# Tokens on partitions and 512-column moving weights in the feed-forwards of a two-model stack

## Chip, cores and metric

The kernel runs on one core of a Trainium2 chip. The time is device microseconds for one launch; three runs gave 2978.11 to 2979.29 us, median 2978.93. All names and lines below are those of the kernel before.

## What is computed

Two layers of one transformer-like block, then its final norm, then two layers of a second block, on 256 tokens of width 1024, all in float32.

```python
def rms_norm(x, g):
    xf = x.astype(jnp.float32)
    y = xf * lax.rsqrt(jnp.mean(xf * xf, axis=-1, keepdims=True) + EPS)
    return (y * g.astype(jnp.float32)).astype(x.dtype)
def swiglu(h, w_gu, w_down):
    gate, up = jnp.split(h @ w_gu, 2, axis=-1)
    return (jax.nn.silu(gate) * up) @ w_down
# first block, per layer (D_FF = 2816)
x = x + 0.5 * swiglu(rms_norm(x, ffn1_norm[l]), ffn1_w_gu[l], ffn1_w_down[l])
z = rms_norm(x, mix_norm[l]) @ w_in[l]   # dilated attention, HGRN2 recurrence, two gates
x = x + merged @ w_mix_out[l]
x = x + cross_attention(rms_norm(x, xattn_norm[l]), rms_norm(mem, mem_norm[l]), ...)
x = x + 0.5 * swiglu(rms_norm(x, ffn2_norm[l]), ...)
# second block, per layer: mod = silu(c) @ w_ada + b_ada gives nine rows of shift, scale, gate
x = x + 0.5 * g1 * swiglu_2(modulate(rmsnorm(x, norm_g[0]), sh1, sc1), ...)
x = x + g2 * (o @ w_out)                 # o: three attentions on a second projection
x = x + 0.5 * g3 * swiglu_2(modulate(rmsnorm(x, norm_g[2]), sh3, sc3), ...)
```

## The kernel before

Everything is transposed: the residual `x` is held as features on the 128 partitions, 8 blocks `k` of 128 features by 256 tokens. All weights come as one stream of 438 tiles of 128 x 2048 floats (1 MB). The queue SP loads tile `p` into a ring of four when tile `p-4` is done. `high` (L278, ACT) rounds it to `w_hi` (three buffers, so it waits until tile `p-3` is done), `low` (L287, DVE) writes the remainder over the ring. `triple` (L295, PE) makes each product from three fp32r matmuls (high x high, high x low, low x high). A tile is 48 matmuls: `project` (L310) has the weights as the stationary 128 x 128 operand and 256 tokens as the moving one; `project_tok` (L321) the reverse, with 256 weight columns moving. Each ends with a count on `tile_done`, which frees the ring.

A norm: `square` on ACT, `norm_pe` (ones-matmul over the 8 blocks, L366), Ln and Exp on ACT, a correction step `refine` on DVE over all 256 tokens, then scaled, high and low parts in quarters (`norm_dve` L393, `split_act` L354). PE waits for the first quarter of the next `h_hi`, `h_lo`.

A feed-forward (`ffn_pe` L425) has 11 chunks of 256 inner columns, 33 tiles: gate and up of chunk `i`, then down of chunk `i-1`. The inner product `g_f`, `g_hi`, `g_lo` is made by DVE (`gated` L541) in the transposed layout that down wants. The four output banks are cleared by zero matmuls and added to for the whole feed-forward. In seven of the eight DVE also does the modulation product (`ada_product` L487) with tiles that POOL loads. There are eight feed-forwards (FFN_A, FFN_B in each layer of the first block, FFN_C, FFN_D of the second). In FFN_B of both layers the rstd is applied late, to gate and up.

After FFN_A comes the mix. Its tiles are M_F (forget, 4), M_Q (4), M_I (value, 4), M_QK and so on. The evacuation of the fourth M_F tile starts a list on DVE (L1221 to L1264: reciprocal, scale, scan, arguments of the decay), with `low` calls written in between by hand; the order of every queue is written out in the code. After FFN_C comes Z_QI, ahead of each FFN_D the out projection Z_O, and the cross attention has M_OUT ahead and X_O behind.

## Time and profile before

| | |
|---|---|
| median of three runs | 2978.93 us |
| profiled execution | 2977.7 us, its span 2975.7 us |
| mean granted clock of PE | 0.985 of full speed |
| PE busy | 2874.4 us, 97% |
| DVE busy | 2036.3 us, 68% |
| ACT busy | 1315.9 us, 44% |
| DMA | 551 MB, mean 185 GB/s |

PE is TensorE, PEld its weight load, DVE VectorE, ACT ScalarE, POOL GpSimd, SP the queue that loads the stream. A busy PE is not PE at its peak, since matmul records overlap: the start-to-start distance tells the rate.

### The profile page before, as it was taken

What the parts mean: (1) busy time and instruction counts of PE and PEld (TensorE: products, weight loads), DVE (VectorE), ACT (ScalarE), POOL (GpSimd) and SP (SyncE); (2) the same over time, 40 slices, a digit from 0 to 9 for tenths busy, and PEclk for the clock granted to TensorE, in tenths of its full rate; (3) what the DMA queues carried; (4) which work ended last, traced back from release to release, by engine and by line L of the source; (5) the groups of instructions that cost most, each with busy time, mean ns of one, the idle gap of its engine ahead of it and who ended that gap; (6) DMA issues with size and microseconds to landing.
All of it is one profiled execution on the core that took longest, in us unless ns stands there. A gap on an engine that the chain in (4) does not pass through costs nothing.

```text
span 2975.7 us, 51299 instructions
## 1 busy us (share of the span) xinstructions
PE 2874.4 (97%) x22844; PEld 2806.2 (94%) x22844; DVE 2036.3 (68%) x2287; ACT 1315.9 (44%) x1303; POOL 206.6 (7%) x166
## 2 busy tenths in 40 slices
PE   7999999999999999999999998998999999999999
PEld 7999999999999999999999998997889999987999
DVE  6677876556677677876656776667866676778644
ACT  5334545444334344545444334335643343446432
POOL 0000420000000000420000000003000000030000
PEclk9999999999999999999999999999999999999999
DMA  7664433445665754433445665663246656542454
GB/s 274 240 227 156 155 125 133 154 148 202 241 241 212 250 204 170 142 134 123 163 148 214 243 238 184 241 227 128 86 178 246 236 215 253 184 141 72 156 183 143
DMA packets 79035, 551.09 MB, mean 185 GB/s; under 512 B 8544, under 2 KB 12000, under 8 KB 12896
## 3 DMA queue, kind: packets, MB, share of 16 engines
q1 hardware_dynamic: 67152, 464.98, 43.6%
q0 software_dynamic: 11664, 82.84, 7.3%
q8 instruction: 180, 2.95, 0.4%
q14 instruction: 39, 0.32, 0.0%
HBM read 546.74 MB, written 1.05 MB: 184 GB/s over the span
## 4 chain that ended last, share of the span: by engine, by line
PE 80%; DVE 13%; ACT 3%; issue 2%; POOL 2%; DMA 0%; DVEq 0%; POOLq 0%; SPq 0%; ACTq 0%
PE ps L298 73%; DVE ring_lo L292 3%; ACT w_hi L285 2%; PE ps L370 1%; PE ps L770 1%; POOL qk L1520 1%; DVE hk L1223 1%; POOL rope_a L1516 1%; DVE e L375 0%; PE ps L900 0%; PE ps L1610 0%; DVE e L1281 0%; DVE e L1280 0%; DVE e L397 0%; DVE a_hg L1301 0%
## 5 line engine op out<-in xcount | busy, mean ns | idle before, releaser
L292 DVE TENSOR_TENSOR ring_lo<-ring,w_hi 128x2048 fp32r<-128x2048 f32 x438 | 1009.5, 2307 | 649.2 <-ACT w_hi L285 645.6
L298 PE MATMUL ps<-h_hi,w_hi 128*128 128x256 f32 x4560 | 1312.5, 288 | 52.0 <-DVE h_lo L407 27.5
L298 PE MATMUL ps<-h_lo,w_hi 128*128 128x256 f32 x4560 | 1298.7, 285 | 0.0
L298 PE MATMUL ps<-h_hi,ring_lo 128*128 128x256 f32 x4560 | 1298.1, 285 | 0.0
L285 ACT ACTIVATE w_hi<-ring 128x2048 fp32r<-128x2048 f32 x438 | 836.7, 1910 | 807.5 <-PE ps L298 631.3
L298 PEld LDWEIGHTS ps<-h_hi,w_hi 128*128 128x128 f32 x4560 | 883.8, 194 | 63.7 <-issue 55.6
L298 PEld LDWEIGHTS ps<-h_lo,w_hi 128*128 128x128 f32 x4560 | 884.6, 194 | 2.9 <-issue 2.4
L298 PEld LDWEIGHTS ps<-h_hi,ring_lo 128*128 128x128 f32 x4560 | 883.8, 194 | 0.0
L298 PE MATMUL ps<-g_hi,w_hi 128*128 128x256 f32 x1408 | 398.5, 283 | 0.0
L298 PE MATMUL ps<-g_lo,w_hi 128*128 128x256 f32 x1408 | 398.5, 283 | 0.0
L298 PE MATMUL ps<-g_hi,ring_lo 128*128 128x256 f32 x1408 | 398.5, 283 | 0.0
L298 PEld LDWEIGHTS ps<-g_hi,w_hi 128*128 128x128 f32 x1408 | 270.3, 192 | 0.0
L298 PEld LDWEIGHTS ps<-g_lo,w_hi 128*128 128x128 f32 x1408 | 270.3, 192 | 0.0
L298 PEld LDWEIGHTS ps<-g_hi,ring_lo 128*128 128x128 f32 x1408 | 270.3, 192 | 0.0
L496 DVE CUSTOM_DVE_ANT_0 e<-e,val 128x1024 f32<-128x1024 f32 x154 | 181.9, 1218 | 0.0
L523 ACT ACTIVATE g_f<-ps 128x512 f32<-128x512 f32 x66 | 39.5, 598 | 209.5 <-PE ps L298 209.5
L298 PE MATMUL ps<-w_hi,h_hi 128*128 128x256 f32 x448 | 130.7, 292 | 0.0
L298 PE MATMUL ps<-ring_lo,h_hi 128*128 128x256 f32 x448 | 128.2, 286 | 0.0
L298 PE MATMUL ps<-w_hi,h_lo 128*128 128x256 f32 x448 | 128.1, 286 | 0.0
L484 POOL DMA_DIRECT2D e<-ada x77 | 40.6, 528 | 1205.8 <-DVE mod_sum L496 1049.4
L550 DVE TENSOR_TENSOR g_f<-g_f,ps 128x512 f32<-128x512 f32 x88 | 60.5, 687 | 69.6 <-PE ps L298 68.9
L298 PEld LDWEIGHTS ps<-w_hi,h_hi 128*128 128x128 f32 x448 | 87.6, 196 | 1.6 <-issue 1.6
(316 smaller groups left out, 3164.7 us busy)
## 6 DMA issues: line engine op xcount, KB each, us to landing
ring<-stream SPq DMA_DIRECT2D x438, 1024.0 KB, 4.8
...
```

The lines of the kernel that those rows point to most:

```text
L285: nc.scalar.activation(w_hi[:, p % HIGHS, :], ring[:, p % RING, :], ACT.Copy).then_inc(S.w_hi_ready, 1)
L292: nc.vector.tensor_tensor(ring_lo[:, p % RING, :], ring[:, p % RING, :], w_hi[:, p % HIGHS, :].bitcast(F32), ALU.subtract).then_inc(S.w_lo ...
L298: mm = nc.tensor.matmul(out, a, b, start=start and n == 0, stop=stop and n == 2, skip_group_check=group)
L370: mm = nc.tensor.matmul(ps[:, bank, 0:T], ones, sq[:, k, :], start=(k == 0), stop=(k == KD - 1))
L484: pool.dma_start(e_buf[(i + 1) % 2][:].rearrange("p k t -> p (k t)"), ada[l * 2 * PER_FFN + first + i]).then_inc(ada_loaded[(i + done) % 2 ...
L496: ins = nc.vector.tensor_tensor_reduce(part, part, silu_c, 1.0, 0.0, ALU.mult, ALU.add, mod_sum[:, at + n:at + n + 1])
L523: nc.scalar.activation(g_f[:, i % 2, :], ps[:, i % 2, :], ACT.Silu).then_inc(S.silu_done, 1)
L550: nc.vector.tensor_tensor(g_f[:, b, :], g_f[:, b, :], ps[:, 2 + b, :], ALU.mult).then_inc(S.hidden_step, 1)
L770: mm = nc.tensor.matmul(ps[:, 4 + 2 * g + j // 2, at:at + n], sta[:, hd, t * P:(t + 1) * P], right, start=True, stop=True)
L1223: ins = nc.vector.reciprocal(hk[:, hd, :], hk[:, hd, :])
L1516: nc.gpsimd.tensor_tensor(rope_a[:], part, cos1[:].unsqueeze(1).broadcast_to([P, 2, T]), ALU.mult).then_inc(S.pool_chain, 1)
L1520: nc.gpsimd.tensor_tensor(part, rope_a[:], turned[n % 2][:], ALU.add).then_inc(S.rope_done, 1)
```

## The change

`x` is held as two blocks of 128 tokens on partitions, 1024 features each, and so is the output. A norm sums squares within a partition (`accum_out`), rstd is one column per block, and gains, shifts and gates are rows broadcast to all partitions by POOL's DMAs (from memory; the modulation vector is written there first by `send_mods`). The scaled block is transposed by PE (`flip_x`, four 128 x 128 per half-row), copied to `h_hi` by ACT (`h_high`) and `h_lo` by DVE (`h_low`). All 256 tokens are no longer treated at once: block 0 runs ahead of block 1 (`cross_act`, `cross_dve`, `first_pair`, and `after` in `ffn_pe`).

In feed-forwards, the value projection and the out projections the activations are stationary and 512 weight columns move; a tile now holds 4 of 8 `k` blocks for 512 columns (`by_halves`), and two tiles make a projection. Gate and up of a chunk share a bank. The inner product comes out with tokens on partitions and is transposed by PE (`flip`), then split. The zero matmuls go. `out_pairs` does an out projection so: both blocks for the first 512 columns, then block 0, then block 1 for the rest. In the mix two value tiles go ahead of M_F, two stay behind M_Q.

The core of the diff, with eight columns of indentation taken off:

```diff
+def cross_act(act, n, base, p, late, ready=None):
+    def sq(q):
+        square(act, n, q, ready and ready[q])
+    sq(0)
+    sq(1)
+    if late:
+        h_high(act, n, 0, base)
+        h_high(act, n, 1, base)
+        nc.scalar.preload_act_table_set("natural_log_exp_and_others")
+        rstd_act(act, n, 0)
+    else:
+        rstd_act(act, n, 0)
+        h_high(act, n, 0, base)
+        h_high(act, n, 1, base)
+    if p >= 0:
+        act.wait_ge(S.tile_done, p + 1)
+    high(act, p + HIGHS)
+    sq(2)
+    sq(3)
+    if not late:
+        rstd_act(act, n, 1)
+    h_high(act, n, 2, base)
+    h_high(act, n, 3, base)
+    if late:
+        rstd_act(act, n, 1)
+    if p >= 0:
+        act.wait_ge(S.tile_done, p + 2)
+    high(act, p + 1 + HIGHS)
+def flip_x(pe, n, b, base):
+    for q in (2 * b, 2 * b + 1):
+        pe.wait_ge(S.h_scaled, nth(S.h_scaled, 4 * n + q + 1))
+        for j in range(4):
+            at = (4 * (q % 2) + j) * P
+            mm = nc.tensor.transpose(ps[:, base + q, j * P:(j + 1) * P], xs[:, b, at:at + P], ident)
+        mm.then_inc(S.xt_done, 1)
...
+def residual(dve, chain, q, bank, scale):
+    part = part_of(x, q)
+    if isinstance(scale, float):
+        nc.vector.scalar_tensor_tensor(out=part, in0=ps[:, bank, :], scalar=scale, in1=part,
+                                       op0=ALU.mult, op1=ALU.add).then_inc(S.x_ready, 1)
+    else:
+        chain(nc.vector.tensor_tensor(part_of(xs, q), ps[:, bank, :], row_of(ROW_GATE, q), ALU.mult))
+        nc.vector.tensor_tensor(part, part, part_of(xs, q), ALU.add).then_inc(S.x_ready, 1)
...
+def cross_dve(dve, chain, n, base, p, late, shift, row_count, into=None):
     def scaled(q):
+        if late:
+            ins = nc.vector.tensor_tensor(part_of(xs, q), part_of(x, q), row_of(ROW_GAIN, q), ALU.mult)
         else:
+            ins = nc.vector.scalar_tensor_tensor(out=part_of(xs, q), in0=part_of(x, q),
+                                                 scalar=rs[:, q // 2:q // 2 + 1], in1=row_of(ROW_GAIN, q),
+                                                 op0=ALU.mult, op1=ALU.mult)
+        if shift:
+            chain(ins)
+            ins = nc.vector.tensor_tensor(part_of(xs, q), part_of(xs, q), row_of(ROW_SHIFT, q), ALU.add)
+        ins.then_inc(S.h_scaled, 1)
+    def add(q):
+        if into:
+            into(q)
+            dve.wait_ge(S.x_ready, nth(S.x_ready, 4 * n + q - 3))
+    def tile_low(i):
+        low(dve, p + i + HIGHS)
+    if row_count == 0:
+        dve.wait_ge(S.first_row, 16)
+    else:
+        dve.wait_ge(S.row_loaded, 16 * row_count)
+    if late:
+        for q in range(2):
+            add(q)
+            scaled(q)
+        h_low(dve, n, 0, base)
+        h_low(dve, n, 1, base)
+        variance(dve, n, 0)
+        rstd_dve(dve, chain, n, 0, True)
+        tile_low(0)
+        for q in range(2, 4):
+            add(q)
+            scaled(q)
+        h_low(dve, n, 2, base)
+        h_low(dve, n, 3, base)
+        variance(dve, n, 1)
+        rstd_dve(dve, chain, n, 1, True)
+    else:
+        for b in range(2):
+            add(2 * b)
+            add(2 * b + 1)
+            if b == 1:
+                tile_low(0)
+            variance(dve, n, b)
+            rstd_dve(dve, chain, n, b)
+            scaled(2 * b)
+            scaled(2 * b + 1)
+            h_low(dve, n, 2 * b, base)
+            h_low(dve, n, 2 * b + 1, base)
+    tile_low(1)
+def first_pair(pe, p, n, base, banks, done=None):
+    pe.wait_ge(S.w_lo_ready, p + 1)
+    for b in range(2):
+        for k in range(KD):
+            if k % 4 == 0:
+                pe.wait_ge(S.h_ready, nth(S.h_ready, 4 * n + 2 * b + k // 4 + 1))
+            if b == 0 and k == 4:
+                pe.wait_ge(S.w_lo_ready, p + 2)
+            if b == 0 and k == 6:
+                flip_x(pe, n, 1, base)
+            mm = triple(ps[:, banks[b], :], both(h2, k, b * P, (b + 1) * P),
+                        weights(p + k // 4, (k % 4) * 512, (k % 4 + 1) * 512), k == 0, k == KD - 1)
+            if b == 1 and k % 4 == 3:
+                mm.then_inc(S.tile_done, 1)
+        if b == 0 and done is not None:
+            mm.then_inc(done, 1)
...
+def ffn_pe(pe, p0, f, n, base, between=None, after=None):
+    def gate_up(i, half, p, b):
+        for k in range(4):
+            mm = triple(ps[:, 2 * (i % 2) + b, :], both(h2, 4 * half + k, b * P, (b + 1) * P),
+                        weights(p, k * 512, (k + 1) * 512), half == 0 and k == 0, half == 1 and k == 3)
+        return mm
+    def flip(i, blocks):
+        for b in blocks:
+            pe.wait_ge(S.prod_done, nth(S.prod_done, 2 * (CHUNKS * f + i) + b + 1))
             for a in range(2):
+                mm = nc.tensor.transpose(ps[:, 2 * (i % 2), a * T + b * P:a * T + (b + 1) * P],
+                                         g_f[:, i % 2, b, a * P:(a + 1) * P], ident)
+        mm.then_inc(S.t_done, 1)
+    def down(i, b, p):
+        for h in range(2):
+            for a in range(2):
+                c = a * T + b * P
+                mm = triple(ps[:, 4 + 2 * b + h, :], both((g_hi, g_lo), i % 2, c, c + P),
+                            weights(p, a * D + h * 512, a * D + (h + 1) * 512), i == 0 and a == 0,
+                            i == CHUNKS - 1 and a == 1)
+            if i == CHUNKS - 1 and 2 * b + h < 3:
+                mm.then_inc(S.down_done, 1)
+        return mm
+    first_pair(pe, p0, n, base, (0, 1), S.gu_done)
+    if between:
+        between()
+    for i in range(1, CHUNKS):
+        p = p0 + 3 * i - 1
+        pe.wait_ge(S.w_lo_ready, p + 1)
+        for b in range(2):
+            mm = gate_up(i, 0, p, b)
+        mm.then_inc(S.tile_done, 1)
+        flip(i - 1, (0, 1))
+        pe.wait_ge(S.w_lo_ready, p + 2)
+        gate_up(i, 1, p + 1, 0).then_inc(S.gu_done, 1)
+        gate_up(i, 1, p + 1, 1).then_inc(S.tile_done, 1)
+        if i < CHUNKS - 1:
+            pe.wait_ge(S.g_ready, nth(S.g_ready, (CHUNKS + 1) * f + i))
+            pe.wait_ge(S.w_lo_ready, p + 3)
+            if i == 1 and f == 0 and between:
+                pe.wait_ge(S.mem_var, 1)
+            for b in range(2):
+                mm = down(i - 1, b, p + 2)
             mm.then_inc(S.tile_done, 1)
+    last, p = CHUNKS - 1, p0 + FFN_TILES - 2
+    flip(last, (0,))
+    pe.wait_ge(S.g_ready, nth(S.g_ready, (CHUNKS + 1) * f + last))
+    pe.wait_ge(S.w_lo_ready, p + 1)
+    down(last - 1, 0, p)
+    pe.wait_ge(S.g_ready, nth(S.g_ready, (CHUNKS + 1) * f + last + 1))
+    pe.wait_ge(S.w_lo_ready, p + 2)
+    down(last, 0, p + 1)
+    flip(last, (1,))
+    down(last - 1, 1, p).then_inc(S.tile_done, 1)
+    if after:
+        after()
+    pe.wait_ge(S.g_ready, nth(S.g_ready, (CHUNKS + 1) * f + last + 2))
+    down(last, 1, p + 1).then_inc(S.tile_done, 1)
...
+    silu(0, 0)
+    tile_high(0)
+    silu(0, 1)
+    tile_high(1)
+    if between:
+        between()
+    if row:
+        silu_row(act, row)
+    for i in range(1, CHUNKS):
+        if i >= 2:
+            tile_high(3 * i - 2)
+        act.wait_ge(S.t_done, nth(S.t_done, (CHUNKS + 1) * f + i))
+        nc.scalar.activation(g_hi[:, (i - 1) % 2, :], ps[:, 2 * ((i - 1) % 2), :],
+                             ACT.Copy).then_inc(S.ghi_ready, 1)
+        tile_high(3 * i - 1)
+        silu(i, 0)
+        silu(i, 1)
+        if i < CHUNKS - 1:
+            tile_high(3 * i)
+    last = CHUNKS - 1
+    for b in range(2):
+        act.wait_ge(S.t_done, nth(S.t_done, (CHUNKS + 1) * f + last + 1 + b))
+        nc.scalar.activation(halves_of(g_hi[:, last % 2, :])[:, :, b * P:(b + 1) * P],
+                             halves_of(ps[:, 2 * (last % 2), :])[:, :, b * P:(b + 1) * P],
+                             ACT.Copy).then_inc(S.ghi_ready, 1)
+        if b == 0:
+            tile_high(3 * last)
+def ffn_dve(dve, l, layers, p0, f, late, products=True, between=None):
+    def gated(i, b):
+        dve.wait_ge(S.silu_done, nth(S.silu_done, 2 * (CHUNKS * f + i) + b + 1))
+        up = ps[:, 2 * (i % 2) + b, T:2 * T]
+        g = g_f[:, i % 2, b, :]
+        if late:
+            ins = nc.vector.scalar_tensor_tensor(out=g, in0=up, scalar=rs[:, b:b + 1], in1=g,
+                                                 op0=ALU.mult, op1=ALU.mult)
+        else:
+            ins = nc.vector.tensor_tensor(g, g, up, ALU.mult)
+        ins.then_inc(S.prod_done, 1)
+    gated(0, 0)
     low(dve, p0 + HIGHS)
+    gated(0, 1)
+    low(dve, p0 + 1 + HIGHS)
     if between:
         between(0)
     if products:
         ada_product(dve, l, layers, PER_FFN * f, 0)
     for i in range(1, CHUNKS):
+        if i >= 2:
+            low(dve, p0 + 3 * i - 2 + HIGHS)
+        dve.wait_ge(S.ghi_ready, nth(S.ghi_ready, (CHUNKS + 1) * f + i))
+        nc.vector.tensor_tensor(g_lo[:, (i - 1) % 2, :], ps[:, 2 * ((i - 1) % 2), :],
+                                g_hi[:, (i - 1) % 2, :].bitcast(F32), ALU.subtract).then_inc(S.g_ready, 1)
+        low(dve, p0 + 3 * i - 1 + HIGHS)
+        gated(i, 0)
+        gated(i, 1)
         if i < CHUNKS - 1:
+            low(dve, p0 + 3 * i + HIGHS)
         if products:
             ada_product(dve, l, layers, PER_FFN * f, i)
         if between:
             between(i)
+    last = CHUNKS - 1
+    for b in range(2):
+        dve.wait_ge(S.ghi_ready, nth(S.ghi_ready, (CHUNKS + 1) * f + last + 1 + b))
+        at = (slice(None), slice(None), slice(b * P, (b + 1) * P))
+        nc.vector.tensor_tensor(halves_of(g_lo[:, last % 2, :])[at], halves_of(ps[:, 2 * (last % 2), :])[at],
+                                halves_of(g_hi[:, last % 2, :])[at].bitcast(F32),
+                                ALU.subtract).then_inc(S.g_ready, 1)
+        if b == 0:
+            low(dve, p0 + 3 * last + HIGHS)
...
+    first_pair(pe, MIX, 1, 4, (0, 1))
+    for n in range(2, 10):
         if n >= 3:
             pe.wait_ge(S.evac_done, nth(S.evac_done, n - 2))
-        (project_tok if n >= 8 else project)(pe, MIX + n, n % 3, h2)
+        project(pe, MIX + n, n % 3, h2)
+    for half in range(2):
+        project_half(pe, M_I1 + half, half, (10 % 3, 11 % 3), h2, 8)
...
-    ffn_dve(dve, l, 0, FFN_A, 0, between=once if l == 0 else None)
-    residual(dve, ffn_banks(dve, FFN_A, 0), 4, 0.5,
-             lambda b: gains(dve, 4, v_now[:, V1_MIX:V1_MIX + KD], b))
-    low(dve, MIX - 2 + HIGHS)
-    norm_dve(dve, chain, 1)
-    low(dve, MIX - 1 + HIGHS)
+    ffn_dve(dve, l, 0, FFN_A, 0, True, between=once if l == 0 else None)
+    cross_dve(dve, chain, 1, 4, FFN_A + FFN_TILES - 2, False, False, 4 * l + 1,
+              with_ready(dve, chain, ffn_ready(dve, FFN_A, 0), 4, 0.5))
     chain(nc.vector.tensor_copy(lb_now[:, 1, :], lb[:, l, :]))
     chain(nc.vector.tensor_scalar(lb_now[:, 0, :], lb_now[:, 1, :], -1.0, 1.0, ALU.mult, ALU.add))
     for n in range(4):
-        low(dve, M_F + n + HIGHS)
-    dve.wait_ge(S.evac_done, nth(S.evac_done, 4))
+        low(dve, MIX + n + HIGHS)
+    dve.wait_ge(S.evac_done, nth(S.evac_done, 6))
     chain(nc.vector.tensor_scalar(hk[:], hk[:], 1.0, None, ALU.add))
...
-    norm_pe(pe, 0, e_buf[0])
-    ffn_pe(pe, FFN_C, 0, 0)
-    norm_pe(pe, 1, e_buf[0])
+    if l == 0:
+        flip_x(pe, 0, 0, 4)
+    ffn_pe(pe, FFN_C, 0, 0, 4, after=lambda: flip_x(pe, 1, 0, 4))
+    flip_x(pe, 1, 1, 4)
```

## Rows read from the trace of the kernel before

**Rows 1.** The page: busy time of each engine.

```profile
PE 2874.4 (97%) x22844; PEld 2806.2 (94%) x22844; DVE 2036.3 (68%) x2287; ACT 1315.9 (44%) x1303; POOL 206.6 (7%) x166
```

**Rows 2.** The page: GB/s in 40 slices; engines' shares of the last chain.

```profile
GB/s 274 240 227 156 155 125 133 154 148 202 241 241 212 250 204 170 142 134 123 163 148 214 243 238 184 241 227 128 86 178 246 236 215 253 184 141 72 156 183 143
...
PE 80%; DVE 13%; ACT 3%; issue 2%; POOL 2%; DMA 0%; DVEq 0%; POOLq 0%; SPq 0%; ACTq 0%
```

**Rows 3.** Chain of waits, whole span: start us, length us, what, instructions.

```profile
21.10 7.86 PE ps L298 x48
...
216.91 3.47 PE ps L370 x16
...
225.03 25.53 PE ps L298 x192
...
720.88 184.31 PE ps L298 x1536
...
1792.79 3.47 PE ps L370 x16
...
1810.89 191.93 PE ps L298 x1584
...
2002.82 3.47 PE ps L370 x16
...
2011.42 13.58 PE ps L298 x96
...
2771.74 3.47 PE ps L370 x16
...
2780.34 191.94 PE ps L298 x1584
```

**Rows 4.** Groups by shape: count | busy us, mean ns | idle before.

```profile
L298 PE MATMUL ps<-h_hi,w_hi 128*128 128x256 f32 x4560 | 1312.5, 288 | 52.0 <-DVE h_lo L407 27.5 <-DVE h_lo L403 20.0 <-DVE ring_lo L292 2.6
...
L292 DVE TENSOR_TENSOR ring_lo<-ring,w_hi 128x2048 fp32r<-128x2048 f32 x438 | 1009.5, 2307 | 649.2 <-ACT w_hi L285 645.6
...
L285 ACT ACTIVATE w_hi<-ring 128x2048 fp32r<-128x2048 f32 x438 | 836.7, 1910 | 807.5 <-PE ps L298 631.3 <-DMA ring<-stream 176.0
...
L370 PE MATMUL ps<-e,con_sb 128*128 128x256 f32 x240 | 57.9, 396 | 12.9 <-ACT e L343 12.9
...
L343 ACT ACTIVATE e<-x 128x512 f32<-128x512 f32 x60 | 36.6, 625 | 34.0 <-DVE x L600 17.2 <-DVE x L604 14.0 <-DVE x L1536 2.8
...
L600 DVE SCALAR_TENSOR_TENSOR x<-ps,x 128x512 f32<-128x512 f32 x32 | 22.1, 692 | 28.4 <-PE ps L298 27.5
...
L348 ACT ACT_TABLE_LOAD x15 | 19.2, 1283 | 0.3
```

**Rows 5.** Timeline, PE, behind a gap: start us, length us, instruction.

```profile
2194.86 0.41 PE L298 MATMUL ps<-h_lo,w_hi 128*128 128x256 f32 x1
2195.07 0.41 PE L298 MATMUL ps<-h_hi,ring_lo 128*128 128x256 f32 x1
```

**Rows 6.** Timeline, a norm's matmuls ahead of the second block's layer 1.

```profile
2387.01 3.62 PE L370 MATMUL ps<-e,con_sb 128*128 128x256 f32 x16
```

**Rows 7.** Chain of waits, the list of DVE in the mix.

```profile
256.48 4.98 DVE hk L1223 x3
...
295.50 2.21 DVE ring_lo L292
...
297.85 11.76 PE ps L298 x96
```

**Rows 8.** Chain of waits, 440 to 700 us: four transposes.

```profile
645.20 0.44 PE ps L911 x4
```

**Rows 9.** The ring's DMAs: landing times.

```profile
DMA to landing us min/median/max: 4.6/4.8/13.0
```

**Rows 10.** Instructions on the tile prob: reading the accumulator.

```profile
L1129 ACT ACTIVATION_READ_ACCUMULATOR prob<-prob,small x16: 186/187/188, 639.7 to 1551.2; 128x1 f32 x16
```

More of the change, by code:

```diff
@@ L94, in tiles_1 @@
     at = l * TILES_1
-    return [at + t for t in (FFN_A, MIX, M_F, M_Q, M_I, M_QK, M_OG, M_YB, M_YA, M_KV0, M_OUT, M_KV1, X_Q, X_V, X_O,
+    return [at + t for t in (FFN_A, MIX, M_F, M_Q, M_I1, M_QK, M_OG, M_YB, M_YA, M_KV0, M_OUT, M_KV1, X_Q, X_V, X_O,
                              FFN_B)]
@@ L134 @@
 VEC_LB = VEC_2 + DEPTH * V2_W
[L135 to L136 removed]
+VEC_INV = VEC_LB + DEPTH * KD
 VEC_W = VEC_INV + 1
@@ L477, in ada_pool @@
+        def ada_pool(pool, l, first, done, free, row=False, then=None):
             for i in range(PER_FFN):
@@ L503, in silu_row, with ffn_act, silu, tile_high @@
             nc.scalar.activation(silu_c, silu_c, ACT.Silu).then_inc(S.silu_row, 1)
-        def ffn_late_act(act, p0, f, n, row):
-            for t in range(FFN_TILES - 1):
+        def ffn_act(act, p0, f, late, between=None, row=None):
+            def silu(i, b):
+                if late is not None and i == 0:
+                    act.wait_ge(S.rs_ready, 2 * late + b + 1)
+                if b == 0:
+                    act.wait_ge(S.gu_done, nth(S.gu_done, CHUNKS * f + i + 1))
+                else:
+                    act.wait_ge(S.tile_done, p0 + (2 if i == 0 else 3 * i + 1))
+                nc.scalar.activation(g_f[:, i % 2, b, :], ps[:, 2 * (i % 2) + b, 0:T], ACT.Silu,
+                                     scale=1.0 if late is None else rs[:, b:b + 1]).then_inc(S.silu_done, 1)
+            def tile_high(t):
@@ L1314, in one_dve @@
             args(0)
-            for n in range(1, 4):
-                low(dve, M_I + n + HIGHS)
+            for n in range(9, 12):
+                low(dve, MIX + n + HIGHS)
             for i in range(LEVELS + 1):
@@ new lines, in final_act @@
+        def final_act(act):
+            nc.scalar.preload_act_table_set("natural_log_exp_and_others")
+            for b in range(2):
+                square(act, 0, 2 * b)
+                square(act, 0, 2 * b + 1)
+                rstd_act(act, 0, b)
+        def final_dve(dve, chain):
+            dve.wait_ge(S.row_loaded, 16 * (4 * DEPTH + 2))
+            for b in range(2):
+                variance(dve, 0, b)
+                rstd_dve(dve, chain, 0, b)
+                for q in (2 * b, 2 * b + 1):
+                    nc.vector.scalar_tensor_tensor(out=part_of(x, q), in0=part_of(x, q), scalar=rs[:, b:b + 1],
+                                                   in1=row_of(ROW_GATE, q), op0=ALU.mult,
+                                                   op1=ALU.mult).then_inc(S.x_ready, 1)
@@ L2120, in ahead @@
                     vectors_two(chain, l + 1)
-            def first_gains(b):
-                if l < DEPTH - 1:
-                    gains(dve, 12, parts[1], b)
-            ffn_dve(dve, l, DEPTH, FFN_D, 1, products=l < DEPTH - 1, between=ahead)
-            residual(dve, ffn_banks(dve, FFN_D, 1), 4, parts[8], first_gains)
+            low(dve, Z_O + HIGHS)
+            low(dve, Z_O + 1 + HIGHS)
+            cross_dve(dve, chain, 2, 0, Z_O + 2, False, True, row_count + 6,
+                      with_ready(dve, chain, z_ready, 0, None))
@@ L2129, in two_pool @@
+            ffn_dve(dve, l, DEPTH, FFN_D, 1, False, products=l < DEPTH - 1, between=ahead)
+            into = with_ready(dve, chain, ffn_ready(dve, FFN_D, 1), 4, None)
+            if l < DEPTH - 1:
+                cross_dve(dve, chain, 3, 4, FFN_D + FFN_TILES - 2, False, True, row_count + 9, into)
+            else:
+                dve.wait_ge(S.row_loaded, 16 * (row_count + 7))
+                for q in range(4):
+                    into(q)
         def two_pool(pool, l):
+            sent = 1 + 3 * l
```

775 lines of the change are left out of this document (346 added, 429 removed).

## Prediction

> **What bounds the kernel now.** I read the totals first: PE is busy for 2874 of 2975.7 us, DVE for 2036, ACT for 1316 [rows 1]; the chain that ended last gives PE 80% and DVE 13% [rows 2]. So PE's rate and PE's gaps are what a change can win. Three things are to be seen.
>
> The rate: in a feed-forward 1536 matmuls of 256 columns take 184.31 us, 0.1200 us each, no gap between them [rows 3]. A tile of 1 MB is 48 of them, 5.76 us. Each has its own weight load beside it, and a record lasts 288 ns, so they overlap [rows 4]. Is 0.120 the stream of 256 columns, or the load of the 128 x 128 operand? Two rows say the load. At the low clock (1.2 GHz) the same matmuls start 0.21 us apart [rows 5], which is 256 columns at one a cycle with nothing added. And where a record streams twice as long, the sixteen of L370, the last starts about 3.62 - 0.40 = 3.22 us after the first [rows 4, 6]: 0.215 us each, 0.213 of it columns.
>
> The gaps: between streams PE stands about 5 us and spends 3.5 on the ones-matmul of the norm. Norm to stream takes 216.91 to 225.03 (8.1 us), 2002.82 to 2011.42 (8.6), 2771.74 to 2780.34 (8.6), and 18.1 where the final norm lies between two blocks (1792.79 to 1810.89); the streams behind them are 1.9 to 2.5 us longer than their count at 0.120, in part at the low clock [rows 3, 5]. Five more gaps repeat these patterns.
>
> The projections after the first feed-forward of each layer: PE is hardly idle, but DVE's list (reciprocals L1223, scan, weight remainders) runs from the end of the four forget tiles, 225.03 + 25.53 = 250.6, to the remainder for tile MIX+12, which ends at 297.7, and PE starts that tile at 297.85 [rows 7]. That wait ends last there.
>
> **The change, part by part.** The sum is made against the profiled execution, 2977.7 us.
>
> 1. *512 columns.* 296 of the 438 tiles (8 x 33 of the feed-forwards; 8 value tiles; 24 of the out projections) go from 48 x 0.120 to 24 matmuls. Bounds for one: 0.215 [rows 6] and 0.240, twice the 256-column pace [rows 3]. I take 0.216, near the lower end, as its row has the same stream length beside a load. 7104 x 0.024 = -170.5 us. Fixed cost of 0.0133 per matmul instead would make it 0.227 (+76 us on my sum).
> The Trainium skill, "TensorE: Matmul & The Clock Gate", section "Back-to-back issue gap", gives N/2.4 + 2.5 ns for one matmul behind another: 215.7 ns at 512, which the trace's 0.215 fits, but 109 ns at 256, where the trace has 120. Its section on LDWEIGHTS puts a load at P/1.2, 107 ns, which would not hold a 256-column stream back; by that rule the extra 11 ns would be a cost per matmul and the gain would be the smaller one (about 2965 us).
>
> 2. *Transposes of the inner part.* 4 per chunk, 44 per feed-forward, 352 in all. Four take 0.44 us between matmuls of other kinds [rows 8]: 352 x 0.109 = +38.3 us, all on PE, nothing hides them. Bounds 0.107 and 0.13 a piece: 37.7 to 46.
> The wait on them is covered in the steady part: flip(i-1) wants a product finished 10 us before, and its copy (0.6) and remainder (0.7) lie under the second half of gate-up, 5.2 us. Per chunk (15.98 us) DVE has three remainders 6.9, two products 0.9, one g_lo 0.7, the modulation product 2.6 = 11.1, ACT 7.1. Weight tiles: load to landing 4.8, at most 13.0 [rows 9], high 1.91, low 2.3 [rows 4], in 3 x 5.18 = 15.6 us. Covered, except at the longest landings.
>
> The stream's rate rises from 4 MB in 17.28 us (243 GB/s) to 4 MB in 15.98 (262 GB/s); a slice with more, 274, stands in the page [rows 2]. New on POOL's queue are the rows for gain, shift and gate (0.5 MB each, one to three ahead of a crossing, in the block's second half behind a write of the modulation vector to memory), issued a feed-forward chunk or a dozen microseconds before DVE waits for them; a 1 MB load lands in 4.8, so I take nothing. If that cover is gone, a crossing waits up to one landing, 13 us [rows 9]. SP's queue keeps its order apart from the start, where weight tile 0 now goes ahead of half of x.
>
> 3. *End of a feed-forward.* DVE does gated(10,1), the modulation product (2.6) and only then g_lo of block 0, which down(10,0) waits for: DVE is free 3.7 us after gate-up ends, g_lo at 4.2, PE arrives at 2.9. Stall 1.3, in 7 of 8.
>
> 4. *Crossings.* The norm matmuls and the 5 us waits go; 16 transposes (1.75 us) come, and block 1 must be waited for in the middle of first_pair. I follow each queue in its order, prices from [rows 4]: residual 0.69, square 0.63 + accumulator 0.19 [rows 10], single-column steps 0.1 to 0.3 each, 1.3 together, scale 0.69. With t=0 at the end of down(10,0), feed-forward to mix:
> DVE must first do g_lo of block 1, which needs flip(10,1): 1.25. Residuals 2.65, square 3.5, rstd 4.8, scaled 5.45 and 6.15. PE has finished down(9,1) at 2.85 and waits 2.6; transposes; down(10,1) ends at 9.25, not 5.4. Block 1: residuals to 10.15, the weight remainder low(MIX+1), which the code puts ahead of the variance, to 12.45, rstd 13.6, scaled 14.3 and 15.0. PE does k 0-3 by 11.85, waits for that remainder, k 4-5 to 13.8, waits, transposes, and ends the pair at 22.0, against 5.4 + 10.4 bare. Overhead 6.2 + 1.3 = 7.5; before 8.1 + 2.5 = 10.6.
> The same bookkeeping, with these differences: *late* form (layer 0's last feed-forward to layer 1's first) scales at once but has table load 1.28 and high(tile 1) in front of k=4: 6.8 against 9.6, -2.8. *Gate and shift rows* (second block) double the residual and the scaling: 12.7 against 11.2 into FFN_C of layer 1; Z_O to FFN_D 13.0 against 10.5, twice. *FFN_C to Z_QI* has no first_pair to lie under: PE is through down(10,1) at 12.2 and block 1 is transposed only at 20.7; start 21.0, then 2.3 at the low clock: 19.2 against 10.7, +8.5, twice. *Final norm*: 18.2 against 20.0, -1.8. The crossings of M_OUT and X_O lie partly under other projections before and after; I take their sum as unchanged, +-3 each. *Start*: the tables' chain of DVE (7 us) moves from ahead of the first matmul to behind the first pair; first matmul about 16.5 instead of 21.1 [rows 3], but down(0) then waits for g_lo: +3. *End*: the last residual has two ops: +0.6.
> Sum without the mix: -2.8 +1.5 +5 +17 -1.8 +3 +0.6 = +22.5.
>
> 5. *Order of the mix.* Two value tiles are now ahead of the forget tiles, and DVE's list starts at the sixth evacuation. The list keeps its length: about 47.9 us from the last forget tile to low(MIX+12), Ln now behind tile MIX+10. From the bare end of the feed-forward: 1.3 + 3.85 + first pair 12.75 + four tiles 23.0 + 47.9 + two tiles 11.5 = 100.3 to the first level; before 216.91 to 309.6 = 92.7 [rows 3, 7]. +7.7 per layer, though four tiles there got shorter (4 x 0.576, which item 1 has credited already): +20 for both. PE's stalls appear at MIX+7 (3.2), MIX+8 (1.3), MIX+12 (9).
>
> Sum: 2977.7 - 170.5 + 38.3 + 22.5 + 20 = 2888. The runs' median is 1.2 above the profiled execution: **2889**. So the tiles give and about half of it is handed back.
>
> **Rivals.**
> A. *The block order pays in full*: each crossing costs its transposes and 2 us, no more. The nine gaps cost 104 us before, with the lengthened streams behind them; they would cost 9 x 3.75 = 34, a gain of 70 where my sum has a loss of 13 (-6.2 for the two ahead of the mix is inside its +20): 2889 - 83 = 2806. For it: the diff lets block 0's chain run under 5 us of matmuls. Against it: the chain I add up is longer than the cover, and part of it sits behind low() and g_lo on DVE. With only part of it, 2835.
> B. *A per-matmul cost*, 0.227: 2965. For it, the 13 ns at 256; against, the row of L370 [rows 6].
> C. *Crossings worse*: longer waits drop PE to the low clock more often (a first tile there takes 2.1 to 2.5 more [rows 3]); eight more of them and 1 to 2 us each: 2910 to 2935.
> D. *Slower than before*: the 512-column stream keeps the 256-column rate, 0.240 each. Then item 1 is nothing, and transposes and crossings remain: 2978 + 38 + 42 = 3059. It decides from 0.2286 us per matmul upwards (80.8/7104 = 0.0114 below 0.240). Against it: 0.21 at the low clock shows one column a cycle.
>
> **How the numbers follow.** Forecast 2889, its own range 2865 to 2915: 0.55. A (whole or part) 0.19, C 0.13, B 0.07, D 0.05, no change 0.01. The range 2835 to 2935 leaves out the lower half of A, B and D, about 0.2 together. Under 0.2% (6 us) no measurement here tells from no change; faster is the forecast, A, C and nearly all of B: 0.93; within 0.2% 0.02; slower D, 0.05.
>
> **What would show it.** Feed-forward matmuls 0.216 apart and 33 tiles plus transposes in about 176 us; PE's first tile of the mix ahead of a DVE list that ends where PE waits at MIX+7 and MIX+12; PE idle near 8 us ahead of Z_QI, with the low clock behind it; residual of block 0 on DVE behind g_lo. Wrong would be: starts 0.227 or more apart, or crossings in which PE waits less than 2 us.

## The result, and the profile after

The changed kernel takes 2990.1 us against 2978.2 us of the kernel before, five runs each: a ratio of 1.0043, 95% interval 1.0028 to 1.0058. It is slower, by more than the 0.2% that can be told from no change, where 2889 was forecast. The profiled execution spans 2987.7 us.

From the page: busy time of each engine, and the engines' shares of the chain that ended last.

```profile
PE 2817.1 (94%) x16040; PEld 2449.9 (82%) x16040; DVE 1976.3 (66%) x2205; ACT 1374.4 (46%) x1550; POOL 224.4 (8%) x197
...
PE 75%; DVE 15%; ACT 5%; issue 2%; DMA 2%; POOL 2%; SPq 0%; DVEq 0%; ACTq 0%; POOLq 0%
```

Beside [rows 1, 2]: PE does 57 us less with 6804 fewer records, and the span is 12 us longer, so PE stands about 70 us more. ACT, DMA and DVE have a larger share of the chain. A triple of matmuls is now L304, high L291, low L298, a transpose of the inner product (`flip`) L593, one of the scaled block ahead of a projection (`flip_x`) L406.

The rate, from the chain of waits (start us, length us, what, instructions), and the group of 512-column matmuls (count | busy us, mean ns of one):

```profile
777.05 16.38 PE ps L304 x72
793.86 16.36 PE ps L304 x72
```

```profile
L304 PE MATMUL ps<-w_hi,h_hi 128*128 128x512 f32 x1600 | 638.7, 399 | 11.9 <-DVE ring_lo L298 10.8 <-DVE h_lo L456 0.7
```

A chunk of a feed-forward is three tiles, 72 matmuls, and four transposes: 793.86 - 777.05 = 16.81 us, 16.36 / 72 = **0.2272 us** a matmul and 0.44 for the four. [Rows 3] had 17.28 for the same work; 15.98 was forecast. No gap lies inside these streams.

The waits of PE (released by: total us, times, longest):

```profile
PE ps L406 <- DVE e L470: 49.8, 22, 8.7
PE ps L304 <- DVE ring_lo L298: 36.2, 13, 9.2
PE ps L406 <- DVE e L463: 17.6, 5, 15.7
PE ps L304 <- DVE g_lo L750: 14.4, 5, 5.1
PE ps L406 <- DVE e L465: 8.4, 6, 2.5
PE ps L304 <- DVE g_lo L765: 4.6, 7, 0.7
```

L406 waits are the crossings (the stretch from one projection's last product through the residual and norm to the next one's first), 15.7 of them the start. The ring_lo waits are mostly the mix (3.4 and 9.3 in each layer). L765 is the end of a feed-forward. L750 is the first down product of a feed-forward (5.1, 2.1, 1.1, 2.9 and 3.2, in five of the eight), and the forecast had no such wait apart from the start. The chain through one of them, layer 0's second feed-forward:

```profile
732.47 8.83 DMA ring<-stream
...
741.41 1.92 ACT w_hi L291
...
743.36 0.97 DVE ring_lo L298
...
745.57 1.22 DVE e L667
...
747.94 0.61 DVE g_lo L750
...
748.60 11.22 PE ps L304 x48
```

Block order keeps weight tile p0 of the first pair in use until block 1 has passed through it (732.45). Only then is tile p0+4 asked for, and the first down product wants it 14 us later, at 746.5 (the pair's last twelve matmuls 2.7, gate-up 10.9, four transposes 0.4). It lands in 8.8, its high takes 1.9 and its remainder 2.3, and DVE does the modulation product (2.4) ahead of g_lo (0.6): 16 us, and PE starts at 748.6.

A crossing in which DVE sets the pace, FFN_C to Z_QI, on the same chain (1994 to 2030 us):

```profile
2006.15 1.11 PE ps L406 x4
2007.26 4.13 PE ps L304 x12
...
2012.93 2.29 DVE ring_lo L298
...
2019.36 1.11 PE ps L406 x4
...
2020.59 9.51 PE ps L304 x66
```

PE stands 4.6 us ahead of block 0's transposes and 6.6 ahead of block 1's, and between them runs twelve matmuls in 4.13 us, not 2.73. The stretch's row (window, us, busy time and records of PE and PEld, DVE, ACT, POOL, then the granted clock) has 0.67 for them, so a part of them runs at 1.2 GHz:

```profile
2007.30:2011.40 4.10, 4.08 (x12) 2.83 (x11) 2.08 (x3) 2.48 (x3) 0.00 (x0) 0.67 0.01 2
```

From the end of down(10,0) (1994.13 + 2.73) to Z_QI it is 23.7 us.

### The profile page after: what moved, and what is told of

The parts are those of the page before. It is cut to its first block, busy times and chain, and to the rows that moved or that the text cites. A ratio compares the mean times of both kernels' runs of the same rounds, so it can differ in the third digit from the quotient of the medians.

```text
span 2987.7 us, 37668 instructions
## 1 busy us (share of the span) xinstructions
PE 2817.1 (94%) x16040; PEld 2449.9 (82%) x16040; DVE 1976.3 (66%) x2205; ACT 1374.4 (46%) x1550; POOL 224.4 (8%) x197
## 4 chain that ended last, share of the span: by engine, by line
PE 75%; DVE 15%; ACT 5%; issue 2%; DMA 2%; POOL 2%; SPq 0%; DVEq 0%; ACTq 0%; POOLq 0%
PE ps L304 68%; DVE ring_lo L298 4%; ACT w_hi L291 2%; DMA ring<-stream 2%; PE ps L593 1%; POOL qk L1671 1%; PE ps L942 1%; DVE e L667 1%; PE ps L406 1%; DVE e L465 1%; POOL rope_a L1667 1%; DVE e L470 1%; DVE x L431 0%; PE ps L1071 0%; PE ps L1097 0%
## 5 line engine op out<-in xcount | busy, mean ns | idle before, releaser
L298 DVE TENSOR_TENSOR ring_lo<-ring,w_hi 128x2048 fp32r<-128x2048 f32 x438 | 1012.2, 2313 | 567.8 <-ACT w_hi L291 567.2
L291 ACT ACTIVATE w_hi<-ring 128x2048 fp32r<-128x2048 f32 x438 | 836.8, 1911 | 382.7 <-PE ps L304 304.8
L304 PE MATMUL ps<-w_hi,h_hi 128*128 128x512 f32 (+1 forms) x1920 | 732.9, 382 | 11.9 <-DVE ring_lo L298 10.8
L304 PE MATMUL ps<-w_hi,h_lo 128*128 128x512 f32 (+1 forms) x1920 | 719.7, 375 | 0.0
L304 PE MATMUL ps<-ring_lo,h_hi 128*128 128x512 f32 (+1 forms) x1920 | 719.4, 375 | 0.0
L304 PE MATMUL ps<-h_hi,w_hi 128*128 128x256 f32 x1488 | 434.9, 292 | 25.6 <-DVE ring_lo L298 25.4
L304 PEld LDWEIGHTS ps<-w_hi,h_hi 128*128 128x128 f32 x1920 | 365.9, 191 | 80.3 <-issue 19.7
L304 PE MATMUL ps<-h_lo,w_hi 128*128 128x256 f32 x1488 | 425.6, 286 | 0.0
L304 PE MATMUL ps<-h_hi,ring_lo 128*128 128x256 f32 x1488 | 425.5, 286 | 0.0
L304 PEld LDWEIGHTS ps<-w_hi,h_lo 128*128 128x128 f32 x1920 | 365.6, 190 | 65.1
L304 PEld LDWEIGHTS ps<-ring_lo,h_hi 128*128 128x128 f32 x1920 | 366.3, 191 | 61.6 <-issue 1.4
L304 PEld LDWEIGHTS ps<-h_hi,w_hi 128*128 128x128 f32 x1488 | 290.5, 195 | 31.5 <-issue 30.7
L304 PE MATMUL ps<-w_hi,g_hi 128*128 128x512 f32 x704 | 282.4, 401 | 19.0 <-DVE g_lo L750 14.4
L304 PEld LDWEIGHTS ps<-h_lo,w_hi 128*128 128x128 f32 x1488 | 290.7, 195 | 2.7 <-issue 2.4
L304 PEld LDWEIGHTS ps<-h_hi,ring_lo 128*128 128x128 f32 x1488 | 290.2, 195 | 0.0
L304 PE MATMUL ps<-ring_lo,g_hi 128*128 128x512 f32 x704 | 278.2, 395 | 0.0
L304 PE MATMUL ps<-w_hi,g_lo 128*128 128x512 f32 x704 | 277.8, 395 | 0.0
L304 PEld LDWEIGHTS ps<-w_hi,g_hi 128*128 128x128 f32 x704 | 135.0, 192 | 51.5 <-DVE g_lo L750 16.5
L304 PEld LDWEIGHTS ps<-w_hi,g_lo 128*128 128x128 f32 x704 | 134.5, 191 | 29.1
L304 PEld LDWEIGHTS ps<-ring_lo,g_hi 128*128 128x128 f32 x704 | 135.1, 192 | 27.4
```

What stands on the lines that cost most here:

```text
L291: nc.scalar.activation(w_hi[:, p % HIGHS, :], ring[:, p % RING, :], ACT.Copy).then_inc(S.w_hi_ready, 1)
L298: nc.vector.tensor_tensor(ring_lo[:, p % RING, :], ring[:, p % RING, :], w_hi[:, p % HIGHS, :].bitcast(F32), ALU.subtract).then_inc(S.w_lo ...
L304: mm = nc.tensor.matmul(out, a, b, start=start and n == 0, stop=stop and n == 2, skip_group_check=group)
```

## Experiments

Theory: what is missing is the pace. The 13 ns that a 256-column matmul takes above its columns stay at 512 columns, and the rest comes from waits of order, in lists and queues, not of work. Rivals: the streams are held by memory or by the other engines, not by the matmul's form; the losses come from the length of DVE's lists, whatever their order.

**The matmul by itself (pace).** Streams in one kernel with nothing beside them, as:

```
for i in range(48):
    nc.tensor.matmul(ps[:, 1, 0:256], sta(r, i), r[:, 1, 0:256], start=i == 0, stop=i == 47)
```

with sta(r, i) the i-th of eight operands of 128 x 128, in turn.

> Matmuls alone: ten streams of 24 to 72 matmuls behind each other, operands of random data in SBUF, no other engine at work; everything else of the kernel is left out, so only starts are read and not the time. What is the 0.0133 us above the columns in a 256-column fp32r matmul? Theory (a cost of every matmul, hidden at the low clock): fp32r 512 columns 0.227 apart, 384 0.173, 256 0.120, 128 0.067. Rival of my forecast (the load of the 128 x 128 operand holds the 256-column stream at 0.120 and nothing is added to a longer one): 128 columns 0.120 too, 512 columns 0.215, the 0.227 of the changed kernel then being memory traffic of the other engines. With the same stationary operand each time: 0.213 if the cost is the change of operand, 0.227 if it is the type or the instruction. bf16 with 512 columns: 0.216 if the cost belongs to fp32r, 0.227 if to every matmul.

Chain of waits. The ten streams are, in order, fp32r 512 columns (from cold, not shown), 256, 128, 384, 512 with one operand, bf16 512, 256, fp32 256, 512 (two records for each matmul), fp32r 512 (10.94 for 48, not shown):

```profile
28.36 5.75 PE ps L60 x48
34.11 5.31 PE ps L62 x48
39.42 8.37 PE ps L64 x48
47.80 10.92 PE ps L66 x48
...
58.79 10.31 PE ps L68 x47
69.09 5.24 PE ps L70 x48
74.33 10.36 PE ps L72 x48
84.69 20.60 PE ps L74 x48
```

fp32r: 0.1198 at 256 columns, 0.1106 at 128, 0.1744 at 384, 0.2275 at 512, the same with one operand (it is loaded each time). Against one column a cycle at 2.4 GHz that is 13 to 14 ns on top at 256, 384 and 512. bf16: 0.2146 (48 matmuls in 10.30) and 0.1092, 1 to 3 ns on top. The fp32 record of 256 columns takes 0.2158. So 0.227 is the matmul's own, with no other engine at work, and the row that my 0.216 rested on, [rows 6], is of fp32 matmuls by the ones operand: it streams 512 cycles and doesn't carry what fp32r carries. At 128 columns the theory failed: it had 0.067, and the stream stays at 0.1106, as if the load held it (the next run looks closer). That is below the 0.120 at 256 columns, so the load alone doesn't hold those.

**Where the 13 ns sit (pace2).** The same with one thing changed in each stream.

> Matmuls alone again, streams of 48 on random data, all else left out: where do the 13 ns of an fp32r matmul of 256 columns (0.1198 for 0.1067) come from? If from the operand's load (its columns or rows), 64 operand columns or 64 rows give 0.107 to 0.113. If from accumulating in one PSUM bank, four banks in turn give 0.109. If from reading the same moving columns again, four places in turn give 0.109. If it belongs to every fp32r matmul, all four stay at 0.120, a stream of 160 columns shows 0.0667 + 0.013 = 0.080 or the floor of 0.1106 measured at 128 columns, and fp32r and bf16 in turn show the mean of both, 0.1145. The same stream at the low clock at the start: 0.213 if the 13 ns are hidden there, 0.227 or 0.240 if they are a time or cycles of their own. bf16 with 128 columns: 0.053 to 0.056 if no load is in the way, 0.107 to 0.111 if the floor is the load.

Order: fp32r 256 from cold (not shown), 512; 256 with 64 operand columns, with 64 rows, into four banks in turn, from four places in turn; then fp32r and bf16 in turn (one piece each, not shown), 160 columns, bf16 with 128, fp32r 256 (not shown):

```profile
16.59 10.90 PE ps L60 x48
27.49 5.45 PE ps L62 x48
32.94 5.95 PE ps L64 x48
38.89 5.94 PE ps L66 x48
44.83 5.76 PE ps L68 x48
...
56.45 5.33 PE ps L73 x48
61.78 2.70 PE ps L75 x48
```

64 operand columns: 0.1135, 6.9 ns on top for 13. 64 rows 0.124, four banks 0.124, four places 0.120: no gain. 160 columns take 0.111, the floor again, and bf16 goes down to 0.0563 at 128. What fp32r pays goes with the columns of its operand: as a floor of 0.111 for short streams, and as 13 ns that stay in the open under a long one. That it is the load itself is argued and not shown, since 64 operand columns also halve the rows of the result. fp32r and bf16 in turn took 0.244 a pair, 0.122 on average, not the mean of 0.1145: the mixture costs more, and the rows don't tell which of the two pays. The start of the first stream, meant to show the low clock, can't: its matmuls go 0.213 to 0.214 apart (seven in 1.50 us, six in 1.28) where the row of windows has a granted clock of 1.00.

The Trainium skill, "TensorE: Matmul & The Clock Gate", "Back-to-back issue gap", has N/2.4 + 2.5 ns, which it calls the gap of a matmul by itself. The bf16 streams agree (109.2 and 214.6 ns); fp32r doesn't, and there the measurement decides. The page's section "Weight-path perf modes — Fast Weight Load (FWL) and DoubleRow" says the fast load is used with 128 weights and a type that isn't FP32. A floor of 111 ns for fp32r and none for bf16 at 128 columns agrees with that if fp32r counts as FP32 there, which the page doesn't say.

At the low clock nothing stands on top. Timeline of the changed kernel in the crossing to Z_QI (start us, length us, instruction), and the row of windows for it:

```profile
2007.92 0.63 PE L304 MATMUL ps<-w_hi,g_lo 128*128 128x512 f32 x1
2008.34 0.63 PE L304 MATMUL ps<-w_hi,g_hi 128*128 128x512 f32 x1
```

```profile
2008.10:2009.00 0.90, 0.90 (x4) 0.71 (x3) 0.53 (x1) 0.90 (x1) 0.00 (x0) 0.50 0.04 9
```

From 2007.49 to 2009.62 five of them start 0.426 apart at a granted clock of 0.50, which is 512 columns at 1.2 GHz. So [rows 5], which I read as "nothing added", said nothing of the full clock.

**The width undone (split).**

```
-  mm = nc.tensor.matmul(out, a, b, ...)
+  for c in (0, T):
+      mm = nc.tensor.matmul(out[:, c:c + T], a, b[:, c:c + T], ...)
```

Two sums then lie open side by side in a bank, and the kernel leaves out that they come out right; only its times are read.

> The changed kernel with every 512-column matmul as two of 256 columns against the same stationary operand: 7104 more matmuls, nothing else moved. Theory (0.0127 us per 512-column matmul is all that the width gives): +90 us on 2990, 3080, and a chunk of a feed-forward at 17.7 us for 16.8. Rival 1 (the streams are held by memory or the other engines, not by the matmul's form): within 10 us of 2990. Rival 2 (a slower stream covers loads and the vector engine's lists at the start of feed-forwards): +60, 3050.

3061.0 us, ratio 1.028 (1.0265 to 1.0296): +71. A chunk takes 17.71 (17.27 for 144 matmuls, 0.1199 each), so 7104 x 0.0126 = 90 is there as a stream. The waits for g_lo at the first down product fall from 14.4 to 8.9 us, and matmuls at the low clock lose nothing. The span of its profile is 77 longer. Theory upheld, with a part of rival 2: the width is worth some 71 to 80 us, not 170.

**The transposes doubled (flips2).**

```
+  for twice in range(2):
       mm = nc.tensor.transpose(ps[:, 2 * (i % 2), ...], g_f[:, i % 2, b, ...], ident)
```

> The changed kernel with each transpose of an inner chunk done twice (352 more). If a transpose costs what stands between the streams, 0.109 us, +38, 3028. If the change between fp32 transposes and fp32r matmuls costs a part of it that a second one in a row doesn't pay, +25 to +30. If waits at the end of the streams had hidden part of them, less than +25.

3025.4 us, ratio 1.0163 (1.0148 to 1.0178): +35, 0.100 us each, between the first two expectations. In its chain eight transposes in a row take 0.87 us where four took 0.44, so the second one costs what the first does, and the forecast's 0.109 stands; where the other 3 us went isn't traced.

**g_hi and g_lo of chunk 0 first (head).** On DVE, and likewise g_hi on ACT ahead of tile_high(1):

```
   gated(0, 1)
+  g_low(1)
   low(dve, p0 + 1 + HIGHS)
   ada_product(dve, l, layers, PER_FFN * f, 0)
   for i in range(1, CHUNKS):
-      g_low(i)
+      if i >= 2: g_low(i)
```

> The changed kernel with the rounded half and the remainder of inner chunk 0 (g_hi, g_lo) ahead of weight tile p0+4 and of the modulation product on ACT and DVE. Theory (DVE's list holds the first down product: the product's 2.4 us and g_lo's 0.6 stand between the landed tile and PE): the waits on g_lo L750, 14.4 us in 5 feed-forwards, fall to the wait for the tile itself, -10 to -14 us in all, 2977 to 2980. Rival (what is late is the load, and the next remainder moves up to be late in its place): -3 to 0, 2987 to 2990.

2977.2 us, ratio 0.9998 (0.9989 to 1.0007): -13, as the theory had it. The same stretch of its chain now has no wait:

```profile
728.78 0.66 PE ps L406 x4
729.43 12.27 PE ps L304 x54
...
742.14 16.35 PE ps L304 x72
```

At the start the wait only moves, as the rival said: PE stands 4.7 us for the remainder of the next weight tile. All waits for remainders go from 36.2 to 42.0 us while the 14.4 of L750 go, so 8.6 of the 13 us are accounted for by waits.

**The second modulation tile held back (adalate).**

```
   free(i)
+  if i == 1:
+      pool.wait_ge(S.t_done, nth(S.t_done, (CHUNKS + 1) * (done > 0) + 1))
```

> The changed kernel with the second modulation tile of each feed-forward (1 MB on POOL's queue) held back until inner chunk 0 is transposed, some 10 us; its product is due 17 us later. Theory (weight tile p0+4 takes 8 to 10 us instead of 4.8 because two modulation tiles are in flight beside it): it lands 2 to 4 us sooner, the waits of 14.4 us for g_lo L750 fall by 6 to 12, 2978 to 2984. Rival (the tile is late because its place in the ring is freed late, or the product on DVE holds PE anyway): the landing stays at 8 to 10 us or the wait stays, within 2 us of 2990.

2971.8 us, ratio 0.9982 (0.9973 to 0.9991): -18, more than the 6 to 12 expected; its profile's span is 13 shorter. DMA issues from 724 to 746 us (KB each, median us from issue to landing), of the changed kernel, then of this one:

```profile
ring<-stream SPq DMA_DIRECT2D x3, 1024.0 KB, 8.8
e<-ada POOLq DMA_DIRECT2D x2, 1024.0 KB, 8.4
```

```profile
e<-ada POOLq DMA_DIRECT2D x3, 1024.0 KB, 7.4
ring<-stream SPq DMA_DIRECT2D x3, 1024.0 KB, 5.7
```

Tile p0+4 lands some 6 us after its place comes free (732.7, its high starts at 738.8), not 8.8, and the waits L750 are gone, except 3.2 us at the start. That is 11.2 us; the rest of the 18 isn't traced. In the changed kernel two modulation tiles, 0.5 MB of c_row and a row (0.5 MB) were in flight beside it.

**The order of the lists in the mix (mix).** DVE's list before and after, in short:

```
-low 3,4,5,6 | +1, recip 0-2, low 7, recip 3-5, low 8, recip 6-7, low 9, scale, max, low 10, low 11, [Ln], scan, args(0), low 12,13,14
+low 3-7 | +1, recip 0-1, low 8, recip 2-5, low 9, recip 6-7, low 10, scale, max, low 11, low 12, [Ln], scan, low 13, args(0), low 14
```

(low n is the remainder of tile MIX+n.) On ACT the table load and Ln go ahead of the wait for tile MIX+10.

> The changed kernel with another order of DVE's and ACT's lists in the first projections of layers 0 and 1: the remainder for tile MIX+7 ahead of the reciprocals, those for MIX+8 to MIX+13 each one or two places earlier, and the table load and Ln ahead of the wait for tile MIX+10. PE's work and all transfers are the same. Theory (only the order of the two lists makes the waits of 3.4 and 9.3 us there): both go, level(0) starts at about 308 instead of 322.7, -12 to -15 us a layer, 2960 to 2966. Rival (the list's length decides, from the last forget tile to the scan, wherever the remainders stand): the wait of 3.4 goes and the one of 9.3 grows to 10 to 12, -1 to -5 in all.

2962.7 us, ratio 0.9945 (0.9932 to 0.9959): -27, as the theory had it. Chain of the changed kernel, then of this one:

```profile
293.81 1.92 ACT w_hi L291
...
295.75 1.28 ACT L1161
...
297.04 1.93 ACT hb L1163
...
298.99 4.43 DVE hb L1397
...
306.41 2.21 DVE ring_lo L298
...
308.76 13.90 PE ps L304 x96
```

```profile
286.74 2.20 DVE ring_lo L298
...
294.76 4.43 DVE hb L1397
...
299.21 2.29 DVE ring_lo L298
```

The scan (L1397) comes 4.2 us sooner, and the table load and Ln no longer stand in the chain ahead of it. PE's waits of 3.4 and 9.3 us are gone; what is left is 0.7 ahead of a weight tile and 1.3 ahead of level(0), which starts at 308.9, not 322.5. Both lists were moved at once, DVE's and ACT's, so their shares aren't told apart.

**The transposes behind the last down product (order).**

```
-  if after: after()
   pe.wait_ge(S.g_ready, ...)
   down(last, 1, p + 1).then_inc(S.tile_done, 1)
+  if after: after()
```

> The changed kernel with block 0's transposes of a crossing behind the last down product of block 1, not ahead of it, in the six crossings where a feed-forward is followed by a norm of its own: PE has 2.7 us of matmuls ready while it stands waiting for those transposes, and block 1's residuals wait for these matmuls. Theory (in a crossing DVE's list is the bound, and the transposes in PE's queue hold up block 1 as well): -5 us in each of the two crossings to Z_QI, -4 from FFN_D to FFN_C, -1 in each of the two to the mix, about +1 from FFN_B to FFN_A: -10 to -16, 2974 to 2980. Rival (the 2.7 us are the cover under which block 0's halves are made, as the block order means it): every crossing loses that cover, +1 to +2.5 each, 2996 to 3005.

2986.3 us, ratio 1.0030 (1.0018 to 1.0042): -4. In the crossing to Z_QI PE's waits are 1.9, 0.7 and 9.2 for 4.6 and 6.6: the same sum. Z_QI starts 21.7 us after down(10,0), not 23.7. From FFN_D to FFN_C the waits are 7.1 for 7.6. From FFN_B to FFN_A it goes the other way: the first down product comes 39.5 us after the start of down(10,0), not 36.7. The -4 itself isn't clear of noise, as the two intervals (1.0018 to 1.0042 and 1.0028 to 1.0058) overlap; the theory's -10 to -16 and the rival's +6 to +15 are both out. Where DVE's list is the bound, PE waits for it with the cover or without; in the one crossing where PE's waits are short (0.4, 1.2 and 0.5 us), the cover was worth 2.8 us.

**The end of a feed-forward (tail).** g_lo of block 0 ahead of the last modulation product; the table load behind g_hi of block 0.

```
   if b == 0:
+      ada_product(dve, l, layers, PER_FFN * f, last)
       low(dve, p0 + 3 * last + HIGHS)
```

> The changed kernel with, at the end of every feed-forward, g_lo of block 0 ahead of the last modulation product on DVE, and the table load for Ln and Exp on ACT behind g_hi of block 0 (before: behind everything, just ahead of the squares). Theory (both stand in the chain of the crossing): the 4.6 us of waits for g_lo go, and 1.3 us per crossing in up to 7 crossings: -8 to -12, 2978 to 2982. Rival (DVE's own list of residuals, scalings and remainders sets the crossing, and the product only moves inside it): -2 to +2, 2988 to 2992.

2984.2 us, ratio 1.0025 (1.0015 to 1.0035): -6, between the two expectations, and by the times alone not clear of noise either. The 4.6 us of waits L765 are gone, the waits at L406 are the same as before (76.5 us for 75.8). So the product was in the way and the table load hardly was.

**All together (combo, best_a, best_b).** combo has the edits of head, tail, mix and order, and in the crossing behind X_O:

```
-cross_act(act, 3, 4, X_O + 2, True)
+cross_act(act, 3, 4, X_O + 2, True, table=False)
```

> The changed kernel with four edits together: g_hi and g_lo of inner chunk 0 first (measured alone: -13), the end of a feed-forward as measured alone (-6) with the table load of the crossing behind X_O taken out too (1.3 each, twice), the order of the lists in the mix, and the transposes behind the last down product. If the waits are separate the gains add: -13 -8 -27 -13 = -61, 2929. If a shorter crossing or mix only lets PE run into the next list of DVE (1974 of some 2930 us busy): about half of the last two is given back, 2945 to 2955.

2938.1 us, ratio 0.9868 (0.9854 to 0.9881): -52, between the two expectations. The four single runs sum to -50 (-13, -6, -27, -4; the expectation had -13 for the last); each is known to some 4 us, so that they add within 2 is in part luck. It beats both kernels: 52 us below the changed one and 40 below the one before. Its waits of PE:

```profile
PE ps L407 <- DVE e L471: 50.0, 24, 9.2
PE ps L304 <- DVE ring_lo L298: 23.1, 14, 4.7
```

PE's waits for weight remainders are down from 36.2. Those in the crossings are nearly what they were, 73 us for 76.

best_a leaves order out and takes adalate in, with one more edit in the crossing to Z_QI; best_b is best_a with order.

```
-   if b == 1: tile_low(0)
    variance(dve, n, b); rstd_dve(dve, chain, n, b); scaled(2 * b); scaled(2 * b + 1)
+   if b == 1: tile_low(0)
```

> The combined kernel (2938) with the transposes of a crossing back ahead of the last down product (measured alone the other way: -4), with the second modulation tile held back (alone: -18, of which -13 may be the wait that the order of g_hi and g_lo already took), and in the crossing to Z_QI the weight remainder behind block 1's scalings, not ahead of its variance. If holding the tile back still takes the 4.7 us wait for a weight tile after the first pair and shorter ones: 2938 + 4 - 8 - 2 = 2932. If it and the order of g_hi and g_lo were two cures for one wait: 2938 + 4 - 2 = 2940.

> The same kernel with the transposes behind the last down product. By the single runs 4 us below best_a: 2928 or 2936. If the transposes' place gains nothing once DVE's list is in the better order, it equals best_a within 2 us.

2940.7 (0.9860 to 0.9893) and 2940.0 (0.9858 to 0.9887): neither differs from combo, as the second expectation of each had it. So holding the modulation tile back and putting g_lo first are two cures for one wait (the longest one for a remainder, 4.7 us in combo, is still 4.8 in best_a), and with the lists mended the place of the transposes makes no difference that shows.

## Why the prediction was wrong

The step that failed is item 1: "I take 0.216, near the lower end, as its row has the same stream length beside a load". The term was nearly twice too large: 7104 x (0.240 - 0.2272) = 91 us, where 170.5 stood. The prediction's own sign of being wrong, starts 0.227 or more apart, is what the trace shows. "Two rows say the load" was the reading behind it, and neither row could say so: one is at the low clock, where nothing is added, the other of fp32, which doesn't pay. The upper bound, 0.240, came from rows of the same type and was the nearer one. Rival B named the right mechanism, a cost per matmul of 0.227, and got a chance of 0.07 and 2965 us; that the time lies 25 above even that comes from the waits in the table below.

Step by step against what was measured, in us:

| step | forecast | measured | off |
|---|---|---|---|
| 512 columns | -170.5 | -90.9 | +79.6 |
| transposes, 352 | +38.3 | 0.44 for four, as forecast | 0 |
| start, to the end of FFN_A | +3 | +7.2, with a wait of 5.1 at the first down product | +4.2 |
| first down product, 4 others | 0 | 14.4 - 5.1 | +9.3 |
| end of a feed-forward, 5 (two more are in the mix) | 1.3 each | 0.56 to 0.74 each, 3.2 in all | -3.3 |
| feed-forward's end to level(0), twice | 100.3 | 103.9 | +7.2 |
| FFN_C to Z_QI, twice | 21.0 + 2.3 | 23.7 + 1.6 | +4.0 |
| FFN_D to FFN_C | 11.4 without the stall | 14.8 | +3.4 |
| FFN_B to FFN_A | 5.5 without the stall | 5.1 | -0.4 |

The start: FFN_A without its last stall ends at 218.8, not 216.9, and its tiles take 5.3 less (792 x 0.0128 - 4.8). To level(0) it is counted from there to 322.65. In the last two rows it is the end of the first pair, less the 16.4 us that PE's work takes after down(10,0). Together +104.0; the time is 2990.1 - 2889 = 101.1 above the forecast. The other -2.9 must lie in crossings that I didn't read step by step (M_OUT, X_O, Z_O, the final norm, the end).

*Item 2* right, by the trace and by doubling.

*"Covered, except at the longest landings"* was false in one place. I counted DMA time against the steady stream and not the moment at which a ring place comes free: first_pair holds tile p0 through both blocks, the next load starts late, and two modulation tiles are beside it. head and adalate each take it away behind the start; at the start 4.7 and 3.2 us of it stay.

*Item 3* right in kind: 0.56 to 0.74 us each for 1.3, and gone in tail.

*Item 4.* The bookkeeping by queue holds where no low clock comes in: to the mix the pair ends 23.0 us after down(10,0), forecast 22.0, and the stall is 0.6 shorter. It falls short where PE stands 4.6 us in the middle: some of the matmuls and transposes behind go at 1.2 GHz, 4.13 us for 2.73, and again behind the second wait. That was rival C's mechanism, worth 7 us in three crossings and not 21 to 46. Of rival A nothing is left. What DVE does for a crossing is longer than its cover, and in order the cover's place moves the whole by 4 us, which isn't clear of noise.

*Item 5.* Stalls forecast 3.2, 1.3 and 9; measured 3.4, none and 9.3. The list is 48.7 us for 47.9. Two tiles behind it took 13.9, not 11.5, at the low clock. What I didn't see is that the order of the lists, not their length, makes these 25 us: mix takes them back without one instruction less.

*Rival D* got the side right for a reason that didn't hold: it wanted 0.2286 or more, and the pace is 0.2272. It decided from a point that assumed my crossings; with 25 us more of waits the change turns at about 0.2255 (0.2272 less 11.9 / 7104). The bounds 0.215 to 0.240 alone span 178 us, and a range of 100 with 0.93 for faster left most of the upper half out.
